# Issuing the layout of group B's bias table beside a score tile of the prompt, in place of during the second projection

## The chip, the cores and the metric

The kernel runs on one core of a Trainium2 chip. The metric is the device time of one execution in microseconds; before the change, three executions took 2215.56, 2209.62 and 2214.93 us, median 2214.93. The core has five engines with a queue of instructions each: TensorE (PE in the profile; PEld is its weight load), VectorE (DVE), ScalarE (ACT), GpSimd (POOL) and SyncE (SP), which here issues DMAs only. 16 DMA engines move the data, whichever queue issued it.

## The reference

One encoder layer, all float32, is applied to two sequences: a prompt of 1024 tokens and a sample of 512, each with 16 learned meta tokens in front.

```python
h = rmsnorm(x, norm1_g)
qa, ka, va, qb, kb, vb = split(h @ w_in)          # 1024 -> 2304 columns
qa, ka, qb, kb = per-head rmsnorm of each
oa = neighbourhood attention(qa, ka, va, rpb_a)   # group A: 8 heads, 2-D window of a 64-wide grid
ob = windowed attention(qb, kb, vb, t5, sink)     # group B: 8 heads, 2 kv heads, +-128 window
x = x + concat(rmsnorm(oa), rmsnorm(ob)) @ w_out
h = rmsnorm(x, norm2_g)
x = x + (silu(h @ w_gate) * (h @ w_up)) @ w_down  # FFN, width 2816
```

In both groups a bias depends on the distance between query and key: in group A a learned table of 15 x 31 offsets for each head, in group B the T5 buckets, with everything beyond 128 masked. In group B there is a sink logit as well. The meta keys are always visible.

## The kernel before

The work runs in stages with a common barrier behind most of them. The tokens lie in three segments of 512: two of the prompt (0 and 1) and the sample (2). The stages are: norm of segment 0, projection 0, norm 1, projection 1, attention of the prompt, norm 2, projection 2, attention of the sample, output projection ("mix"), FFN. Every product of float32 is done as three TensorE products of a high and a low part, so that all operands are split by ScalarE (high) and by VectorE or GpSimd (low).

**Projection** (`project(g)` on each engine, called with 0, 1, 2). Nine iterations: four pairs of query columns, four of keys and values, and one for group B's keys and values. In an iteration SP loads two weight tiles `wraw` of 512 KB (L602), each as soon as the tile before the last in its slot is free; ScalarE makes the high half `wh` (L972), GpSimd the low half `wl` (L796); TensorE multiplies (L354 to L356) and averages squares (L1532); ScalarE evacuates (L999, L1000) and takes the root (L1025); VectorE inverts and scales (L1284, L1294). ScalarE's `body` is the function that the diff touches: in its first iteration (`it == 0`), behind the root, it also issues a layout of a bias table.

**The bias tables.** A bias tile is a sheared copy of a short line of values: row p of it is the line shifted by p. The lines lie in DRAM (`line_a_dram`, `line_b_dram`), and DMAs from DRAM to DRAM write the sheared tables `table_a` (two halves, one for each sequence) and `table_b`, from which the bias of a head is later loaded. `lay_out_a(0)` issues 8 DMAs (L927) in projection 0, `lay_out_b` 2 DMAs (L935; 216 KB in runs of 18 values and 4608 KB in runs of 384) in projection 1, and `lay_out_a(1)` 16 DMAs beside tile 68 of the prompt's attention. All are issued by ScalarE's queue, on which they stand in order with its other instructions.

**Attention.** A sequence has 16 heads, 8 of group A and then 8 of group B; a head of the prompt has 8 tiles of 128 queries, numbered n = 0 to 127 over the sequence, each with two or three blocks of 128 keys. The engines go through the tiles in step: TensorE's scores of tile n+1 (L1576 to L1579) into one of two banks; VectorE adds the bias and finds the maximum (L1326); ScalarE takes the exponential (L1064); TensorE transposes the probabilities (L1583); ScalarE evacuates them as `pth` (`raise_p`, L1073), VectorE makes their low part `ptl` (L1333), and TensorE multiplies them with the values (L1604). ScalarE's order in `attention(seq)` is: exponential n, then what stands beside that tile, evacuation n-1, and in tile 2 of a head the copy of the next head's queries (L1057).

In each head there are side tasks. SP, in its order: the bias load of the next head, the doubling of the next head's queries (L700), and, every second head, the store and the spread of a pair's inverse sums (L705, L710). For group A the bias of a head comes through one buffer `bias_rows` (L684, 576 KB), which GpSimd adds to the mask (`masks`, L832); for group B it is loaded from `table_b` (L692, L694), the first time for head 8 after a wait on the layout's semaphore. GpSimd, in its order: copy of the meta probabilities (L856), `masks` of the next head, low half of the next head's queries (L814), again L856, meta values (L841), and every second head the scaling of a pair (L849). TensorE transposes the copied meta probabilities at L1588.

Of the kernel before, what the change touches and what calls it, by code (L numbers as in the profile page):

```python
# [64 lines left out]
def hybrid_encoder_layer(nc, x_prompt, x_sample, meta_tokens, t5_table, norm1_g, w_in, qn_a_g, kn_a_g,  # L65
# [152 lines left out]
    with ExitStack() as ctx:  # L218
        bank = [ctx.enter_context(nc.psum_tensor(f"bank{i}", [P, 512], F32)) for i in range(8)]

        def sem(name):
            return ctx.enter_context(nc.semaphore(name))
# [13 lines left out]
        line_out = sem("line_out")  # L236
# [98 lines left out]
        def wait(eng, s, v):  # L335

            if not isinstance(v, int) or v > 0:
                eng.wait_ge(s, v)
# [30 lines left out]
        def norm_tiles(g):  # L369

            first = 0 if g == 0 else 5 + 4 * (g - 1)
            src = x_of["sample"] if g == 2 else x_of["prompt"]
            t0 = 0 if g == 2 else g * SEG
            tiles = [(first + i, P, i * P, src[t0 + i * P:t0 + (i + 1) * P, :]) for i in range(4)]
            if g == 0:
                tiles.append((first + 4, META, SEG, meta_tokens[:, :]))
            return tiles
# [541 lines left out]
        def _(act):  # L919
            def lay_out_a(q):  # L920

                R, W = GEO["prompt" if q == 0 else "sample"]
                for c in range(W):
                    src = line_a_dram[3 * q, 0:1, PAD_A + (R - 1) * 3 * W - c:][0]
                    src = bass.AP(src.tensor, src.offset, [[LEN_A, 3 * NA], [-3 * W, R], [1, WIN]])
                    dst = table_a[q].rearrange("k h (r c) j -> (k h) r c j", c=W)[:, :, c, :]
                    act.dma_start(dst, src).then_inc(table_a_out[q], 16)  # L927

            def lay_out_b():

                for k0, n, off in ((0, MK, P - 1), (MK, WIN, LEN_BM + P - 1)):
                    src = line_b_dram[0, 0:1, off:][0]
                    src = bass.AP(src.tensor, src.offset, [[LEN_B, 3 * NA], [-1, P], [1, n]])
                    dst = table_b[:, :, :, k0:k0 + n].rearrange("k h p c -> (k h) p c")
                    act.dma_start(dst, src).then_inc(table_b_out, 16)  # L935
# [38 lines left out]
            def project(g):  # L974
                sq, rt = sq_of[g // 2], rt_of[g // 2]

                def body(it, kind, i):
                    if g == 0 and kind == "kvb":

                        for m, rows, _, _ in norm_tiles(1)[:3]:  # L980
                            norm_root(1, m, rows)
                    normed_slots = (0, 1) if kind == "q" else (0,)
                    j0 = normed_number(g, kind, 0, i)
                    if isinstance(it, int) and it == 0:

                        wait(act, v_turned, 5 * g)
                        wait(act, k_lo, 5 * g)

                    for slot in range(2):
                        us = units(g, kind, slot)  # L990
                        if kind != "kvb":
                            weight_hi(g, it + 1, slot, True)
                        else:
                            act.wait_ge(mm_done, 18 * g + it * 2 + slot + 1)

                        wait(act, normed, j0 - 1 if kind == "q" and slot == 0 and not isinstance(i, int) else j0)
                        if slot in normed_slots:
                            for u0, w, b, _ in us:
                                act.activation(raw[slot][:, u0:u0 + w], b[:, 0:w], ACT.Copy)  # L999
                                op = act.activation(sq[slot][:, u0:u0 + w], b[:, 0:w], ACT.Square)  # L1000
                            op.then_inc(squared, 1)
                        else:
                            wait(act, v_turned, v_number(g, kind, i))
                            n = SEG // len(us)
                            for j, (_, _, b, _) in enumerate(us):
                                src, dst = b[:, 0:n], raw[1][:, j * n:(j + 1) * n]
                                if kind == "kv":

                                    W, rows = (16 if g == 2 else 8), n // GRID
                                    src = src.rearrange("p (r t c) -> p t r c", r=rows, c=W)  # L1010
                                    dst = raw[1][:, 0:SEG].rearrange("p (t r c) -> p t r c", r=8, c=W)
                                    dst = dst[:, :, j * rows:(j + 1) * rows, :]
                                op = act.activation(dst, src, ACT.Copy)
                            if g == 0:
                                src = us[1][2][:, n:n + META].rearrange("p (o c) -> p o c", o=1)
                                op = act.activation(vtm[:, :].rearrange("p (o c) -> p o c", o=8),
                                                    src.broadcast_to((P, 8, META)), ACT.Copy)
                            op.then_inc(v_copied, 1)

                    for slot in normed_slots:  # L1020
                        act.wait_ge(mean_done, j0 + slot + 1)
                        if kind != "q":
                            wait(act, k_lo, v_number(g, kind, i))
                        for u0, w, _, mb in units(g, kind, slot):
                            op = act.activation(rt[slot][:, u0:u0 + w], mb[:, 0:w], ACT.Sqrt, bias=eps[:, :])  # L1025
                        op.then_inc(root_done, 1)
                    if kind != "q":
                        act.wait_ge(v_turned, v_number(g, kind, i) + 1)
                        for src, hi, _ in v_dests(g, kind, i):
                            op = act.activation(hi, src, ACT.Copy)  # L1030
                        if g == 0:
                            c = 4 * P if kind == "kvb" else i * P
                            op = act.activation(vmh[:, bass.ds(c, P)], bank[5][:, 0:P], ACT.Copy)
                        op.then_inc(v_hi, 1)
                        act.wait_ge(normed, j0 + 1)
                        for x, hi, _, _ in k_parts(g, kind, i):
                            op = act.activation(hi, x, ACT.Copy)
                        op.then_inc(k_hi, 1)
                    if isinstance(it, int) and it == 0 and g < 2:

                        with nc.allow_non_contiguous_dma("runs of bias lines"):
                            if g == 0:
                                act.wait_ge(line_out, 16 * 7)
                                lay_out_a(0)
                            else:
                                lay_out_b()

                pairs(act, body)
                if g:
                    phase_end(act, END_OF[f"proj{g}"])  # L1050
# [32 lines left out]
            def attention(seq):  # L1083
                first, end = HEADS_OF[seq]
                n0, n1 = TILES[seq]
                for h in (first, first + 1):
                    stage_q(h, False)
                for n in range(n0, n1 + 4):
                    if n < n1:
                        exponent(n)  # L1090
                    if n == 68:
                        with nc.allow_non_contiguous_dma("runs of bias lines"):
                            lay_out_a(1)
                    pair = pair_beside(n - 1, seq)
                    if pair is not None:
                        rows = 2 * Head(2 * pair).nt
                        act.wait_ge(rt_turned, pair + 1)
                        act.wait_ge(p_turned, min(n, n1))
                        wait(act, rt_stored, 16 * pair)
                        act.activation(rt_sb[0:rows, :], bank[2][0:rows, WIN:WIN + P], ACT.Copy  # L1100
                                       ).then_inc(rt_out, 1)
                    if n % GROUP == 2 and n - 6 >= n0:
                        raise_meta((n - 6) // GROUP)
                    if n0 <= n - 1 < n1:
                        raise_p(n - 1)
                    if n < n1:
                        h, t = where(n)
                        if t == 2 and first < h < end - 1:
                            stage_q(h + 1, True)
                phase_end(act, END_OF[f"att_{seq}"])  # L1110
# [712 lines left out]
```

## Time and profile before

| what | us |
|---|---|
| median of three runs | 2214.93 |
| the profiled execution | 2209.63 |
| its span, first to last instruction | 2207.8 |
| TensorE busy | 1958.6 (89%) |
| VectorE busy | 1051.5 (48%) |
| ScalarE busy | 667.1 (30%) |
| GpSimd busy | 507.5 (23%) |

Mean granted clock of TensorE over the span is 0.94. The last half of the span is the FFN, in which TensorE is busy throughout. Projection 1 lies at about 205 to 335 us, the prompt's attention at 336 to 574, projection 2 at 600 to 722, the sample's attention at 724 to 932.

In a timeline a row gives start and duration in us, engine, line, operation, tile written from tiles read, and in brackets how long the engine sat idle before the row and what ended that. "issue" is time in which it waited for nothing that the profile shows. A letter q behind an engine's name is its queue, which issues DMAs. Of a DMA there are two times: how long the queue took to issue it, and the time from issue to landing.

### The profile page before, as it was taken

To read this page: it belongs to the slowest core of one execution; us is meant where nothing else is said; L and a number is where in the kernel's file an instruction comes from. 1 tells how busy PE (TensorE), PEld (TensorE's weight loads), DVE (VectorE), ACT (ScalarE), POOL (GpSimd) and SP (SyncE) were. 2 spreads that over 40 slices of the span, in tenths; PEclk is the share of its full clock that TensorE was granted. 3 is DMA by queue.
4 is the path that set the end of the run, shared out by engine and by line. 5 is a ranking of instruction groups with operands and counts; after the bars stand their busy time and mean duration, and the time that the engine had idled before them with its cause. 6 is when DMAs were issued, how large, how long until landed. Compare 5 with 4: busy or idle time off the path is not lost.

```text
span 2207.8 us, 28015 instructions
## 1 busy us (share of the span) xinstructions
PE 1958.6 (89%) x9991; PEld 1646.3 (75%) x9991; DVE 1051.5 (48%) x1788; ACT 667.1 (30%) x1373; POOL 507.5 (23%) x405
## 2 busy tenths in 40 slices
PE   5896887979599466599989999999999999999998
PEld 3695567979577465568758888888888888888887
DVE  3565456757455333465553344433433444334336
ACT  3344346757434433333441111111111111111110
POOL 1231324534233432232111111121111111111110
PEclk7998998989799677789999999999999999999999
DMA  3432513343321323240011000011010000110102
GB/s 101 159 114 52 153 48 94 82 145 90 96 78 55 83 71 98 69 155 1 0 48 39 29 28 28 28 40 36 28 38 28 28 28 28 45 31 28 38 9 114
DMA packets 146718, 136.18 MB, mean 62 GB/s; under 512 B 10880, under 2 KB 133232, under 8 KB 146648
## 3 DMA queue, kind: packets, MB, share of 16 engines
q1 hardware_dynamic: 134048, 120.90, 18.2%
q10 hardware_dynamic: 12600, 14.38, 2.1%
q8 instruction: 40, 0.66, 0.1%
q14 instruction: 30, 0.25, 0.0%
HBM read 122.36 MB, written 20.98 MB: 65 GB/s over the span
## 4 chain that ended last, share of the span: by engine, by line
PE 52%; DVE 3%; issue 1%; POOL 1%; ACT 1%; ACTq 0%; POOLq 0%; DVEq 0%
PE bank L354 17%; PE bank L356 17%; PE bank L355 17%; POOL msl L892 1%; DVE h2l L1447 1%; DVE y L1458 1%; DVE h2h L1449 0%; ACT msh L1126 0%; DVE y L1388 0%; PE bank L1604 0%; PE bank L1699 0%; DVE wol L1392 0%; ACT junk L1145 0%; DVE xn L1402 0%; POOL wol L900 0%
## 5 line engine op out<-in xcount | busy, mean ns | idle before, releaser
L1458 DVE TENSOR_TENSOR y<-bank,y 128x512 f32<-128x512 f32 x528 | 359.3, 692 | 305.7 <-PE bank L356 305.7
L354 PE MATMUL bank<-h2h,gh 128*128 128x512 f32 x528 | 208.5, 395 | 7.3 <-DVE h2h L1449 5.5
L354 PE MATMUL bank<-hth,wh 128*128 128x512 f32 (+2 forms) x512 | 200.7, 392 | 8.9 <-POOLq L349 6.9
L354 PE MATMUL bank<-h2h,uh 128*128 128x512 f32 x528 | 206.3, 391 | 2.5 <-POOL ul L912 2.5
L354 PE MATMUL bank<-dh,acth 128*128 128x512 f32 x528 | 205.7, 390 | 2.6 <-issue 2.6
L355 PE MATMUL bank<-h2l,gh 128*128 128x512 f32 x528 | 206.3, 391 | 0.0
L356 PE MATMUL bank<-h2h,gl 128*128 128x512 f32 x528 | 206.2, 391 | 0.0
L356 PE MATMUL bank<-h2h,ul 128*128 128x512 f32 x528 | 206.1, 390 | 0.0
L355 PE MATMUL bank<-h2l,uh 128*128 128x512 f32 x528 | 206.0, 390 | 0.0
L356 PE MATMUL bank<-dh,actl 128*128 128x512 f32 x528 | 205.6, 389 | 0.0
L355 PE MATMUL bank<-dl,acth 128*128 128x512 f32 x528 | 205.6, 389 | 0.0
L796 POOL TENSOR_TENSOR wl<-wraw,wh 128x1024 fp32r<-128x1024 f32 x54 | 131.4, 2438 | 310.7 <-ACT wh L972 310.7
L1467 DVE TENSOR_TENSOR act_f<-bank,act_f 128x512 f32<-128x512 f32 x66 | 45.6, 692 | 319.3 <-PE bank L356 319.3
L912 POOL TENSOR_TENSOR dl<-draw,dh 128x1024 fp32r<-128x1024 f32 x22 | 52.6, 2393 | 611.2 <-ACT dh L1190 611.2
L355 PE MATMUL bank<-htl,wh 128*128 128x512 f32 (+2 forms) x512 | 187.7, 367 | 0.0
L356 PE MATMUL bank<-hth,wl 128*128 128x512 f32 (+2 forms) x512 | 186.9, 365 | 0.0
L1583 PE MATMUL bank<-ident,logit 128*128 128x128 f32 x512 | 138.7, 298 | 7.0 <-ACT logit L1064 7.0
L1284 DVE RECIPROCAL rt_p<-rt_p 128x512 f32<-128x512 f32 (+2 forms) x31 | 87.7, 2843 | 112.8 <-ACT rt_p L1025 112.8
L1216 ACT ACTIVATE acth<-act_f 128x512 fp32r<-128x512 f32 x66 | 41.7, 632 | 324.2 <-DVE act_f L1467 324.2
L1326 DVE CUSTOM_DVE_ANT_0 logit<-bank,bias 128x274 f32<-128x274 f32 (+1 forms) x192 | 100.0, 522 | 77.6 <-PE bank L1579 58.5
L1333 DVE TENSOR_TENSOR ptl<-bank,pth 128x256 fp32r<-128x256 f32 (+1 forms) x192 | 98.4, 513 | 64.2 <-ACT pth L1073 60.8
L354 PEld LDWEIGHTS bank<-hth,wh 128*128 128x128 f32 x512 | 98.5, 192 | 37.4 <-POOL wl L796 8.4
(186 smaller groups left out, 4053.2 us busy)
## 6 DMA issues: line engine op xcount, KB each, us to landing
wraw<-in_w_in SPq DMA_DIRECT2D x54, 512.0 KB, 3.9
graw<-in_w_gate SPq DMA_DIRECT2D x22, 512.0 KB, 3.9
uraw<-in_w_up SPq DMA_DIRECT2D x22, 512.0 KB, 3.9
draw<-in_w_down SPq DMA_DIRECT2D x22, 512.0 KB, 3.4
bias_rows<-table_a SPq DMA_DIRECT2D x16, 576.0 KB, 4.4
bias<-table_b SPq DMA_DIRECT2D x16, 402.0 KB, 3.5
out<-y SPq DMA_DIRECT2D x12, 512.0 KB, 3.1
table_a<-line_a_dram ACTq DMA_DIRECT2D x8, 576.0 KB
```

The costliest lines, as they stand in the source:

```text
L354: pe.matmul(out, lhs[0], rhs[0], start=start, stop=False, skip_group_check=True)
L355: pe.matmul(out, lhs[0], rhs[1], start=False, stop=False, skip_group_check=True)
L356: return pe.matmul(out, lhs[1], rhs[0], start=False, stop=stop, skip_group_check=True)
L796: pool.tensor_tensor(wl[slot][:, :, :], wraw[slot][:, :, :], f32(wh[slot][:, :, :]), ALU.subtract).then_inc(w_lo, 1)
L912: pool.tensor_tensor(lo[:, :, :], rw[:, :, :], f32(hi[:, :, :]), ALU.subtract).then_inc(s_lo, 1)
L1216: act.activation(acth[:, u * SEG:(u + 1) * SEG], act_f[:, u * SEG:(u + 1) * SEG], ACT.Copy).then_inc(act_hi, 1)
L1284: op = dve.reciprocal(rt[slot][:, u0:u0 + w], rt[slot][:, u0:u0 + w])
L1326: dve.tensor_tensor_reduce(logit[:, n % (2 * GROUP), 0:w], bank[n % 2][:, 0:w], H.bias_of(t), -1.0, 3e38, ALU.add, ALU.min, negm[:, h % 2, ...
L1333: dve.tensor_tensor(turned_to(ptl, n), bank[2 + n % 2][:, 0:k * P].rearrange("p (k c) -> p k c", c=P), f32(turned_to(pth, n)), ALU.subtrac ...
L1458: dve.tensor_tensor(yt, down_bank(t, half)[:, :], yt, ALU.add).then_inc(y_add, 1)
L1467: dve.tensor_tensor(a_, UP_BANKS[u][:, :], a_, ALU.mult).then_inc(act_done, 1)
L1583: return pe.transpose(bank[2 + n % 2][:, c * P:(c + 1) * P], logit[:, n % (2 * GROUP), MK + c * P:MK + (c + 1) * P], ident[:, :])
```

## The change

The two DMAs of `lay_out_b` are no longer issued in the first iteration of projection 1, but on the same queue in the prompt's attention, between the exponential of tile n = 12 and the evacuation of tile 11. Nothing else moves.

```diff
-                    if isinstance(it, int) and it == 0 and g < 2:
+                    if isinstance(it, int) and it == 0 and g == 0:
 
                         with nc.allow_non_contiguous_dma("runs of bias lines"):
-                            if g == 0:
-                                act.wait_ge(line_out, 16 * 7)
-                                lay_out_a(0)
-                            else:
-                                lay_out_b()
+                            act.wait_ge(line_out, 16 * 7)
+                            lay_out_a(0)
...
                     if n < n1:
                         exponent(n)
-                    if n == 68:
+                    if n in (12, 68):
                         with nc.allow_non_contiguous_dma("runs of bias lines"):
-                            lay_out_a(1)
+                            if n == 12:
+                                lay_out_b()
+                            else:
+                                lay_out_a(1)
```

## Rows read from the trace of the kernel before

**Rows 1.** Windows view, prompt's attention: stretch, length, engines' busy time, clock, DMA share, GB/s.

```profile
336.00:574.00 238.00, 201.09 (x1832) 197.67 (x1832) 159.72 (x494) 160.21 (x456) 105.90 (x152) 0.93 0.34 98
```

**Rows 2.** Timeline of SP's queue, prompt's attention: start, duration, queue, line, DMA.

```profile
364.36 0.47 SPq L700 DMA_DIRECT2D qs_p0h<-qs_p0h  x1
...
381.41 0.59 SPq L684 DMA_DIRECT2D bias_rows<-table_a  x1
...
454.13 0.48 SPq L700 DMA_DIRECT2D qs_p1h<-qs_p1h  x1
...
481.49 0.48 SPq L700 DMA_DIRECT2D qs_p0h<-qs_p0h  x1
```

**Rows 3.** Timeline of ScalarE, second projection.

```profile
215.66 0.69 ACT L1025 ACTIVATE rt_p<-bank,eps 128x512 f32<-128x512 f32 x1 [4.62 <-PE bank L1532]
215.66 4.09 ACTq L935 DMA_DIRECT2D table_b<-line_b_dram  x2
...
270.55 0.60 ACT L999 ACTIVATE raw<-bank 128x512 f32<-128x512 f32 x1 [3.39 <-DVE qm L1294]
```

**Rows 4.** Landings of weight loads issued at 222 to 230; then of all 54.

```profile
DMA to landing us min/median/max: 17.3/19.2/21.2
...
DMA to landing us min/median/max: 3.7/3.9/21.2
```

**Rows 5.** Timeline of TensorE, second projection.

```profile
222.50 1.12 PE L1532 MATMUL bank<-sq_p,head_mean 128*128 128x512 f32 x2 [1.31 <-ACT sq_p L1000]
...
243.62 2.07 PE L1532 MATMUL bank<-sq_p,head_mean 128*128 128x512 f32 x2 [7.47 <-ACT sq_p L1000]
```

**Rows 6.** Windows view, second projection.

```profile
230.00:240.00 10.00, 6.14 (x26) 4.49 (x24) 4.10 (x2) 0.69 (x1) 0.00 (x0) 0.99 0.79 225
240.00:250.00 10.00, 6.38 (x20) 4.42 (x21) 0.00 (x0) 4.40 (x7) 3.58 (x2) 0.67 0.79 227
```

**Rows 7.** Timeline of ScalarE, third projection.

```profile
617.63 0.69 ACT L1025 ACTIVATE rt_s<-bank,eps 128x512 f32<-128x512 f32 x1 [4.62 <-PE bank L1532]
...
661.21 0.60 ACT L999 ACTIVATE raw<-bank 128x512 f32<-128x512 f32 x1 [3.39 <-DVE qm L1294]
```

**Rows 8.** Timeline of ScalarE, tile 12 of the prompt's attention.

```profile
365.45 0.63 ACT L1064 ACTIVATE logit<-logit,negm 128x402 f32<-128x402 f32 x1
...
366.08 0.47 ACT L1073 ACTIVATE pth<-bank 128x384 fp32r<-128x384 f32 x1
```

**Rows 9.** Timeline of ScalarE, tile 68 of the prompt's attention.

```profile
456.15 13.03 ACTq L927 DMA_DIRECT2D table_a<-line_a_dram  x15
469.27 0.49 ACT L1073 ACTIVATE pth<-bank 128x384 fp32r<-128x384 f32 x1 [13.21 <-issue]
```

**Rows 10.** Timeline of TensorE, prompt's attention.

```profile
368.10 0.32 PE L1604 MATMUL bank<-pth,vh 128*64 128x256 f32 x1
...
393.92 0.27 PE L1588 MATMUL bank<-ident,pmeta 128*64 128x128 f32 x1
...
457.82 0.26 PE L1579 MATMUL bank<-kmeta,qs_p0l 128*128 128x18 f32 x1
470.41 0.48 PE L1604 MATMUL bank<-pth,vh 128*64 128x256 f32 x1 [12.33 <-DVE ptl L1333]
```

**Rows 11.** Timeline of ScalarE's queue, first projection.

```profile
59.80 10.83 ACTq L927 DMA_DIRECT2D table_a<-line_a_dram  x8
```

**Rows 12.** Timeline of GpSimd, prompt's attention, around the masks of head 4.

```profile
386.67 2.40 POOL L832 TENSOR_TENSOR bias<-bias_rows,mask_a 128x256 f32<-128x256 f32 x3 [3.08 <-DMA bias_rows<-table_a]
390.12 2.51 POOL L814 TENSOR_TENSOR qs_p0l<-qm,qs_p0h 64x512 fp32r<-64x512 f32 x2 [1.06 <-ACT qs_p0h L1057]
392.70 0.24 POOL L856 COPY pmeta<-logit 128x64 f32<-128x64 f32 x1
```

**Rows 13.** Landings of the two spreads of sums issued at 380.3, then at 457.2.

```profile
DMA to landing us min/median/max: 3.8/4.0/4.3
...
DMA to landing us min/median/max: 5.4/6.5/7.7
```

## The prediction

> **What bounds the kernel now.** I read the windows view first, then the timelines of the engines in the two stages that the diff touches, then DMA landing times. Over the prompt's attention TensorE is busy 201 of 238 us [rows 1]; this includes the stage's two ends and one large hole, so between them it is the engine that sets the pace, and what stops it is paid nearly in full. The head period is steady: the query copies of heads 2 and 9 were issued at 364.36 and 454.13, seven heads apart, 12.82 us each, 1.60 us a tile [rows 2]. The second projection is set by TensorE too, except in one place: there its clock falls and it waits. That place is the layout of table_b.
>
> **The part that is removed.** ScalarE's queue issues the two DMAs of the layout at 215.66 for 4.09 us together [rows 3], and moves 4.8 MB on the same DMA engines as the weight loads. The two weight loads issued while it ran landed after 17.3 and 21.2 us, where the median of all is 3.9 [rows 4]. The reader should see three losses. ScalarE does nothing else while it issues; TensorE stands 1.31 and then 7.47 us [rows 5]; the granted clock, 0.99 from 230 to 240 and 0.67 in the next 10 us, goes to half at 239.8 [rows 6], with TensorE stopped since 243.62 - 7.47 = 236.15.
>
> The third projection runs the same loop on the same shapes with no layout beside it, so it prices the sum of these. From the square root of the first pair (215.66 before, 617.63 in the third) to the evacuation of the first key and value pair (270.55 and 661.21) it takes 54.89 against 43.58 us [rows 3, 7]. The removal gives back 11.31 us. From below, the two idle rows alone are 8.8 us [rows 5]; what they leave out is the half clock and a smaller wait. I take 11.3, because both ends of the comparison are the same instructions. What is late next is only TensorE's own stream, as in the third projection.
>
> **The part that is added: the issue.** The query copy of head 2 stands in tile 10; with its doubling at 364.36 [rows 2], the exponential at 365.45 is tile 12's [rows 8], and the two DMAs go in behind it, ahead of the evacuation that now starts at 366.08. Tile 68, where the other sequence's table is laid out, has the same place in its head, and shows what follows: the 16 issues end at 469.18, ScalarE goes on at 469.27 and TensorE at 470.41, 1.14 us later [rows 9, 10]. Queued behind the issues on ScalarE are this evacuation of probabilities and the next exponentials; VectorE's low half waits for the evacuation, and TensorE's products with the values for that.
>
> At the old price of 4.09 us the issues of tile 12 end at 369.54, ScalarE goes on at 369.63, TensorE at 370.77. It would have started that product at 368.10 [rows 10]: a loss of 2.7 us. Its two ends: if both issues cost as little as an issue at tile 68, 13.03/15 or 0.87 us, they end at 367.2 and TensorE loses 0.3 us. If they stretch as the eight larger issues of table_a's first half did (10.83/8 or 1.35 us each [rows 11], 1.56 times those of tile 68), 4.09 becomes 6.4 us and the loss 5.0 us. I take 3.0 us: the old duration with a little on top, since the attention's own loads share the DMA engines. Below nothing is excluded: nothing on ScalarE is shortened here.
>
> The hole would be about 2.8 us long. The hole at 236.15 cost the clock 3.8 us after it began; the 1.31 us hole did not cost it [rows 5, 6]. I count no clock loss; if the hole reaches 5 us there is one. Its price is read at tile 68: the next query copy came at 481.49 in place of 454.13 + 12.82, so 14.5 us late, of which 12.3 is idle [rows 2, 10]; 2.2 us are the half clock.
>
> **The part that is added: the transfer.** The 4.8 MB now run beside the attention's loads for some 25 to 35 us from 368 on (in the projection the DMA share was still 0.79 from 230 to 250, up to 34 us after the issue [rows 6]). First use of table_b is head 8 at tile 64, over 80 us later, so its own landing is covered; were it not, the loss would be the whole transfer. The loads that meet it: the doubling of head 3's queries, the store and spread of the first pair's sums, and the bias rows of head 4, issued at 381.41 behind that spread on SP [rows 2]. The last one has a waiter: GpSimd starts its masks at 386.67, having waited 3.08 us for this load, which so lands after some 5.2 us [rows 12]. Behind the masks stand, in GpSimd's order, the low half of head 4's queries (390.12) and the copy of the meta probabilities (392.70, 0.24 long) [rows 12], and TensorE transposes that copy at 393.92 [rows 10]. Between the masks' end (389.07) and 390.12 there is 1.05 us, and behind the copy 0.98: 2.0 us of slack. What the load loses beyond that, TensorE waits.
>
> How late is it? The same spread of sums, issued at 457.2 beside the other table's layout, landed after 5.4 and 7.7 us in place of 3.8 and 4.3 [rows 13]: 1.6 to 3.4 us late. Weight loads, of smaller pieces, lost up to 17.3 us [rows 4]. The bounds for the bias rows are therefore 0 and 16 us late (a landing at 21.2). The spread is the nearest: the bias rows queue behind it, so its 3.4 us is theirs too, and I add little for their own part, for by then most of the layout has gone: 4.0 us late. Loss 4.0 - 2.0 = 2.0 us. Later loads (head 5's rows at some 394 us) meet at most the tail; nothing for these.
>
> The Trainium skill (DMA: Bandwidth & Descriptors, "Queues, rings and completion order") says that each DMA engine takes turns between the queues that have work, a packet at a time, and under "Issuing engines are not separate DMA queues" that issuing from another engine saves only the sequencer's time. That speaks against this change: the bytes move into a stage with loads of its own. Worked out as an estimate from that page, taking turns at most doubles a landing of 5.2 us, so 5.2 us late, 3.2 us lost, and the whole change gives 5.1 us. The weight loads' landings were worse than double; no row shows the taking of turns itself.
>
> **The sum.** -11.3 + 3.0 + 2.0 = -6.3 us. The profiled execution took 2209.63 us (span 2207.8), hence 2203.3. It lies 5.3 us under the median of the three runs shown (2209.62, 2214.93, 2215.56); the same 6.3 us off that median gives 2208.6 us.
>
> **The rivals.**
>
> No collision: the bias rows land within GpSimd's 2.0 us of slack. For it: that is only 0.6 us more than the 1.6 by which the first spread was late. Against it: they queue behind the second, which was 3.4 late. -11.3 + 3.0 = -8.3: 2206.6 us.
>
> A long issue: the two DMAs hold ScalarE for 6.4 us and the hole pulls the clock down. For it: the stretched issues of table_a's first half, and loads in flight; against it: those 8 were queued one behind another. -11.3 + 5.0 + 2.2 + 2.0 = -2.1: 2212.8 us.
>
> Slower: the bias rows of head 4 land as the weight loads did, after 21.2 us. The place is GpSimd's masks for head 4; the price 16 - 2.0 = 14.0 us of TensorE, with the clock at half after it (2.2). -11.3 + 3.0 + 14.0 + 2.2 = +7.9: 2222.8 us. It outweighs the gain from a delay of 8.1 us on, a landing over 13.3 us. For it: the only loads seen beside this very table lost that much. Against it: the spread beside a layout lost at most 3.4, and the layout is partly done when the bias rows come.
>
> The projection doesn't recover: its waits have another cause, and only ScalarE's 4.09 us goes. For it: nothing but that the two wait rows name ScalarE and not the DMA. Then about -4.1 + 5.0 = +0.9: 2215.8 us.
>
> **How the numbers follow.** Forecast 0.54, no collision 0.18, long issue 0.16, slower 0.07, projection not recovered 0.05. I call 0.3% (6.6 us, about what a measurement of this kernel can tell from no change) the bound. No collision lies beyond it; the forecast (own range 3 to 8 us gained) lies just inside it, and nearly half of its weight falls beyond. So faster 0.18 + 0.26 = 0.44. Slower takes its rival and a little of the last one's: 0.08. The rest, 0.48, is the same. The range goes from the no-collision case less half of the runs' spread of 5.9 us (about 2203.5) to the long issue and a little more (2214); the slower rival and the unrecovered projection, 0.12 together, lie outside.
>
> **What would show it.** In the profile after: weight loads of the second projection all near 3.9 us and no clock loss there, 43.6 us between the two instructions compared; a gap of TensorE of about 2.8 us at tile 14 whose releaser is VectorE's low half, with ScalarE's idle put to issue for about 4 us; GpSimd's wait for the bias rows of head 4 longer by 4 us, and a TensorE wait of about 2 us for the meta probabilities' copy or what follows it. It is wrong if the weight loads stay slow, if the issues take well over 5 us, or if other waits (query doubling, head 5's rows) appear in the attention.

## The result and the profile after

20 executions of each kernel were timed side by side: median 2223.73 us (2216.06 to 2228.77) after, 2215.24 (2209.21 to 2221.96) before. The ratio is 1.0029, 95% interval 1.0017 to 1.0041; it is that of the means, 2222.2 and 2215.8 us, while the medians lie 8.5 us apart. The kernel is slower by 0.3%, about 6.4 us, where 6.3 us of gain were forecast. The profiled execution after took 2216.06 us, its span is 2214.3.

Where the time went can be read from SP's queue alone, since SP issues the first load of each stage. The table has the time from the second projection's first streamed weight load to the attention's mask load, from there to the next norm's first load, and so on. The last two columns belong to experiments told below.

| stage, us | before | after | early copy, before | early copy, after |
|---|---|---|---|---|
| second projection | 139.71 | 128.73 | 144.92 | 129.04 |
| prompt's attention | 239.19 | 254.81 | 235.05 | 253.73 |
| norm and third projection | 149.14 | 148.90 | 148.40 | 149.54 |
| sample's attention, to the load of y | 217.09 | 216.89 | 197.51 | 201.38 |

The projection gives 11.0 us back, the attention takes 15.6. (The projection starts 2.3 us later in the profile after, 197.88 for 195.61; the eight profiles of the experiments lie at 196.2 to 200.3, so that is no part of the change.)

The projection is as it should be. Landings of its weight loads in the profile after (issued from 143 to 350), the windows, and the two instructions of ScalarE compared in [rows 3, 7]:

```profile
DMA to landing us min/median/max: 3.7/3.9/5.2
```

```profile
230.00:240.00 10.00, 10.00 (x42) 7.44 (x41) 5.51 (x4) 5.26 (x8) 4.57 (x2) 1.00 0.25 74
240.00:250.00 10.00, 10.00 (x43) 7.62 (x41) 7.56 (x4) 3.07 (x5) 2.66 (x2) 1.00 0.23 63
```

```profile
218.28 0.69 ACT L1025 ACTIVATE rt_p<-bank,eps 128x512 f32<-128x512 f32 x1 [4.61 <-PE bank L1532]
...
261.87 0.60 ACT L999 ACTIVATE raw<-bank 128x512 f32<-128x512 f32 x1 [3.39 <-DVE qm L1294]
```

They are 43.59 us apart, as in the third projection (43.58), and TensorE has no gap in these 20 us, where it had lost over a third of them [rows 6].

In the attention TensorE has three waits that it did not have. The view of waits of the profile after, TensorE, 350 to 410 us (what waited, for what; total, times, longest):

```profile
PE bank L1604 <- DVE ptl L1333: 3.8, 1, 3.8
PE bank L1576 <- issue: 3.6, 1, 3.6
PE bank L1588 <- POOL pmeta L856: 2.4, 1, 2.4
```

The first is the hole behind the issues. ScalarE's timeline shows its cause:

```profile
357.50 0.78 ACTq L935 DMA_DIRECT2D table_b<-line_b_dram  x1
358.03 0.19 ACT L1061 ACTIVATION_READ_ACCUMULATOR logit<-logit,negm 128x1 f32 x1
358.32 4.56 ACTq L935 DMA_DIRECT2D table_b<-line_b_dram  x1
362.98 0.49 ACT L1070 ACTIVATE pth<-bank 128x384 fp32r<-128x384 f32 x1 [4.76 <-issue]
```

The second issue took 4.56 us, the two 5.38, where they had taken 4.09 in the projection [rows 3].

The second wait is put to issue, which means that the profile shows no releaser. SP's timeline and the landing times show one: the doubling of head 3's queries was issued at 375.48 and landed 8.5 us later, at 383.98, and the first scores of head 3 start at 384.11. The two fences are TensorE's timeline with both gaps, and SP's:

```profile
364.12 0.47 PE L1604 MATMUL bank<-pth,vh 128*64 128x256 f32 x1 [3.82 <-DVE ptl L1333]
...
384.11 0.55 PE L1576 MATMUL bank<-kall,qs_p1h 128*128 128x256 f32 x1 [3.60 <-issue]
```

```profile
375.48 0.47 SPq L700 DMA_DIRECT2D qs_p1h<-qs_p1h  x1
376.38 0.83 SPq L705 DMA_DIRECT2D rt_dram<-rt_sb  x1
384.45 1.11 SPq L710 DMA_DIRECT2D rinv_q<-rt_dram  x2
385.61 0.59 SPq L684 DMA_DIRECT2D bias_rows<-table_a  x1
```

The next doublings in the profile after land after 2.8 or 2.9 us. In the same fence the store of 8 KB at 376.38 holds SP until 384.45; in the view of SP's waits it is 7.2 us, before 1.8. Only then could the bias rows of head 4 go out, and they landed after 10.0 us, so that GpSimd waited 13.77 us and finished the copy of the meta probabilities too late, the third wait:

```profile
395.63 2.41 POOL L832 TENSOR_TENSOR bias<-bias_rows,mask_a 128x256 f32<-128x256 f32 x3 [13.77 <-DMA bias_rows<-table_a]
398.12 2.48 POOL L814 TENSOR_TENSOR qs_p0l<-qm,qs_p0h 64x512 fp32r<-64x512 f32 x2
400.66 0.24 POOL L856 COPY pmeta<-logit 128x64 f32<-128x64 f32 x1
```

Both longer gaps also cost the clock. The windows after (the granted clock, as a share of full speed, is the third number from the end):

```profile
360.00:365.00 5.00, 1.18 (x8) 1.06 (x7) 1.49 (x5) 1.89 (x5) 0.47 (x1) 0.74 1.19 112
365.00:370.00 5.00, 5.00 (x31) 5.00 (x30) 3.30 (x11) 2.46 (x9) 2.58 (x4) 0.58 0.78 127
...
380.00:385.00 5.00, 1.40 (x11) 1.29 (x9) 1.94 (x6) 1.16 (x5) 0.24 (x1) 0.79 0.79 246
385.00:390.00 5.00, 5.00 (x31) 5.00 (x32) 2.13 (x7) 1.99 (x6) 0.00 (x0) 0.53 1.07 239
```

The sum is taken from one doubling to the next on SP, 12.82 us apart before [rows 2]: in the profile after they stand at 356.40, 375.48, 394.59, 409.98 and 422.83, so the heads took 19.08, 19.11, 15.39 and 12.85. The excess is 6.3, 6.3 and 2.6 us: the hole of 3.8, the doubling's wait of 3.6 and the bias rows' 2.4. What is left over beside the first two, 2.4 and 2.7 us, is put down to the clock; it is a difference and was not measured by itself.

### The profile page after: what moved, and what is told of

It reads as the page before. It is cut to its first block, busy times and chain, and to the rows that moved or that the text cites. A ratio compares the mean times of both kernels' runs of the same rounds, so it can differ in the third digit from the quotient of the medians.

```text
span 2214.3 us, 28015 instructions
## 1 busy us (share of the span) xinstructions
PE 1964.8 (89%) x9991; PEld 1652.7 (75%) x9991; DVE 1052.2 (48%) x1788; ACT 667.4 (30%) x1373; POOL 508.1 (23%) x405
## 4 chain that ended last, share of the span: by engine, by line
PE 52%; DVE 3%; issue 1%; POOL 1%; ACT 1%; ACTq 0%; POOLq 0%; DVEq 0%
PE bank L354 17%; PE bank L356 17%; PE bank L355 17%; POOL msl L892 1%; DVE h2l L1447 1%; DVE y L1458 1%; DVE h2h L1449 0%; ACT msh L1126 0%; DVE y L1388 0%; PE bank L1604 0%; PE bank L1699 0%; DVE wol L1392 0%; ACT junk L1145 0%; DVE xn L1402 0%; POOL wol L900 0%
## 5 line engine op out<-in xcount | busy, mean ns | idle before, releaser
L354 PEld LDWEIGHTS bank<-h2h,gh 128*128 128x128 f32 x528 | 99.5, 188 | 35.6 <-DVE h2h L1449 10.0
```

Source lines behind the costliest of these rows:

```text
L354: pe.matmul(out, lhs[0], rhs[0], start=start, stop=False, skip_group_check=True)
```

## The experiments

Each was timed in five rounds beside the kernel before, eight kernels in all. A ratio is to the kernel before.

**The two DMAs apart.**

```diff
-                    if n in (12, 68):
+                    if n in (8, 12, 68):
...
-                            if n == 12:
-                                lay_out_b()
+                            if n < 68:
+                                lay_out_b((0,) if n == 8 else (1,))
```

> The small DMA of the layout is issued beside tile 8 and the large one beside tile 12, so that the second no longer stands right behind the first on ScalarE's queue. Theory A (three separate losses in the changed kernel: ScalarE held 5.35 us, with the clock, some 6 us; the doubling of head 3's queries, with the clock, some 6 us; head 4's bias rows 2.4 us): each issue takes about 0.8 us, TensorE stops less than 1 us at tile 14, its clock stays up there; the other two losses stay. The time is about 6 us under the changed kernel, so about that of the kernel before (-3 to +3 us). Rival B (the long issue is itself the transfer's doing: the DMA engines are busy with the attention's loads and take descriptors slowly): the large issue still takes 3 us or more, the hole stays, and the time stays some 4 to 8 us above the kernel before.

Ratio 0.9986 (0.9972 to 1.0): 0 to 6 us faster than before, some 9.5 us under the changed kernel by the two ratios, where 6 were expected; the attention of the profiles is 6.3 us shorter. ScalarE's queue, then TensorE's waits from 350 to 410 us, of this kernel:

```profile
351.88 0.78 ACTq L935 DMA_DIRECT2D table_b<-line_b_dram  x1
...
358.85 0.74 ACTq L935 DMA_DIRECT2D table_b<-line_b_dram  x1
```

```profile
PE bank L1588 <- POOL pmeta L856: 4.1, 1, 4.1
PE bank L1576 <- issue: 2.4, 1, 2.4
```

The large DMA costs 0.74 us to issue when it doesn't follow the small one (3072 runs of 72 bytes; its own 3072 runs have 1536) at once, and the hole (L1604) is gone. Rival B falls: the issue was long because of the DMA ahead of it on its queue. Of the attention's excess 9.3 us are left (248.48 us). The doubling's wait is shorter by 1.2 us, the bias rows' longer by 1.7, a first sign that these two are not added but overlap.

**The query copy earlier, and its control.** Both have the same edit, one on the changed kernel and one on the kernel before.

```diff
-                        if t == 2 and first < h < end - 1:
+                        if t == 0 and first < h < end - 1:
                             stage_q(h + 1, True)
```

> The changed kernel, with the copy of the next head's queries (and so their doubling) in tile 0 of a head in place of tile 2, some 3.2 us earlier. Theory A: the doubling of head 3's queries still lands late (some 8 us), but 3.2 of the 3.6 us that TensorE waited for it are gone, and the clock doesn't fall for it: 5 to 6 us less than the changed kernel, if the early copy costs nothing by itself (its control is the kernel before with the same edit): difference to the control 0 to +2 us. Rival B (TensorE's wait of 3.6 us, which the profile puts to issue, has another cause, such as GpSimd's low half or the scores' banks): the wait stays, and the difference to the control stays at +6 us or more.

> Control for the early copy of the queries: the kernel before, with the copy in tile 0 of a head in place of tile 2. Both theories: no wait in the prompt's attention hangs on this copy, so within 2 us of the kernel before; if ScalarE is pressed at tile 0, up to 5 us slower, which then is taken off the other.

Ratios 0.9921 (0.9907 to 0.9934) and 0.989 (0.9873 to 0.9907). The control was a miss in a welcome way: by its stages, nearly 20 us of its gain lie in the sample's attention (217.09 to 197.51). TensorE's waits at a head's first scores there are for GpSimd's low half of the copied queries, which follows that copy. They fell from 57.5 to 52.3 us, one of 3.6 us that is put to issue went, and the stage's 856 products took 115.6 us in place of 127.1, at a mean granted clock of 0.80 in place of 0.75.

For the question asked, the difference of the two stays at 0.3%, some 7 us, which is what rival B expected; by the table the move here costs 18.7 us in the attention and gives 15.9 in the projection. But the reason is not rival B's. TensorE's waits in the changed kernel with the early copy, 350 to 410 us:

```profile
PE bank L1588 <- POOL pmeta L856: 13.7, 1, 13.7
PE bank L1604 <- DVE ptl L1333: 3.2, 1, 3.2
```

The wait at the first scores (L1576) is gone. The edit moves GpSimd's low half of these queries as well, but in the profile after that was done at 378.11, 2.4 us before TensorE stood, so the wait was for the doubling:

```profile
375.59 2.52 POOL L814 TENSOR_TENSOR qs_p1l<-qm,qs_p1h 64x512 fp32r<-64x512 f32 x2 [5.84 <-ACT qs_p1h L1054]
```

In its place the wait for the copy of the meta probabilities grew from 2.4 to 13.7 us: GpSimd stood 18.52 us for head 4's bias rows. Some 6.3 us of the growth are what TensorE no longer lost ahead of that wait. The rest is that the rows came later still: SP stood 8.6 us at the store (7.2 in the profile after, 1.0 in the control), and the load landed after 13.4 us (10.0 in the profile after, 5.5 in the control). Theory A, three separate losses, falls as to the last two. The doubling's wait lay in the shadow of a later one.

**The bias rows first.** The same kernel, with one change in SP's order.

```diff
+                    if h == 3:
+                        spread_sums(0)
                     if first < h < end - 1:
                         double_q(h + 1)
-                    if h % 2 == 0 and h > first:
+                    if h % 2 == 0 and h > first and h != 2:
                         spread_sums(h // 2 - 1)
```

> The changed kernel with the early copy of the queries, and with head 4's bias rows issued ahead of the first pair's store and spread on SP, not behind them. Theory C (what ends last in the changed kernel's collision is SP's chain for head 4: a store of 8 KB that takes 7 to 9 us beside the layout in place of 1.8, SP standing at it, and the bias rows queued behind; the stalls of TensorE before it only lie in its shadow): the bias rows go out some 10 us earlier, TensorE's wait of 13.7 us for the meta probabilities falls to under 3 us, and the prompt's attention shortens from 253.7 to 237 to 243 us; the time falls 11 to 16 us below the same kernel without this edit. Rival D (the bias rows' own landing beside the layout is what is late, 10 us and more wherever they are issued): the wait stays at 6 us or more and the time falls by less than 8 us.

Ratio 0.9882 (0.9862 to 0.9901); the attention went from 253.73 to 241.83 us. SP's queue, then TensorE's waits from 350 to 410 us:

```profile
371.35 0.59 SPq L684 DMA_DIRECT2D bias_rows<-table_a  x1
374.84 0.34 SPq L705 DMA_DIRECT2D rt_dram<-rt_sb  x1
382.05 1.11 SPq L710 DMA_DIRECT2D rinv_q<-rt_dram  x2
```

```profile
PE bank L1606 <- DVE ptl L1335: 2.8, 1, 2.8
PE bank L1578 <- issue: 1.0, 1, 1.0
```

The bias rows go out at 371.35 in place of 383.67. Their landing still takes 10.3 us, as rival D has it:

```profile
DMA to landing us min/median/max: 10.3/10.3/10.3
```

But they land some 15 us earlier, GpSimd waits 1.05 us for them in place of 18.52, and the 13.7 us are gone. The store still holds SP for 7 us, but nobody waits behind it. Theory C holds for the wait and for the stage (237 to 243 us expected). Two of its points don't. The timed runs gave some 9 us (0.9921 to 0.9882), between its 11 to 16 and rival D's less than 8. And the place behind the store was only half of the lateness: over the control, the store had taken 7.6 us more and the landing 7.9. The new place in SP's order makes room for both. What is left over the control, 6.8 us, holds the hole of the issue (2.8), its clock and a wait of 1.0 for a doubling.

**The hold alone.** The kernel before, with this ahead of tile 12's evacuation and no transfer added:

```diff
+                    if n == 12:
+                        for x in range(18):
+                            act.activation(rt_sb[0:16, :], ident[0:16, :], ACT.Copy).then_inc(held, 1)
+                            act.wait_ge(held, x + 1)
```

> The kernel before (layout in the second projection), with ScalarE held for some 5 to 6 us beside tile 12 by 18 small copies in a chain, and no transfer: the price of the issue alone. Theory A: TensorE stops 3.5 to 4.5 us at tile 14, its clock falls to half afterwards, and the stage takes 5 to 7 us more; +5 to +7 us. Rival (a hold alone is made good, since the engines behind have idle time): +1 to +3 us.

Ratio 1.0032 (1.0019 to 1.0045), 7.1 us; the attention took 247.29 us, 8.1 more. ScalarE's and TensorE's timelines:

```profile
368.57 6.08 ACT L1094 ACTIVATE rt_sb<-ident 16x128 f32<-16x128 f32 x18
```

```profile
375.82 0.48 PE L1609 MATMUL bank<-pth,vh 128*64 128x256 f32 x1 [5.08 <-DVE ptl L1338]
```

A hold of 6.08 us stops TensorE 5.08 us, 1.0 less, about as the prediction took it; the other 3 us are put down to the clock, 0.78 in 370 to 375 us and 0.53 in 375 to 380. The stop and the time lie a little over what was expected, as does the hold. Nothing of it beyond that 1.0 us is made good later, and the rival falls. This hold, 0.7 us longer than the two issues, costs by itself what the whole change cost on balance.

**The layout in pieces.** Eight pieces of 16 rows of every head's table, and the small DMA, each beside a tile in which ScalarE has idle time.

```diff
+                    at_b = [8 * h + x for h in range(5) for x in (5, 7)][:9]
+                    if n in at_b or n == 68:
...
+                                piece_b(8 if n == 5 else at_b.index(n) - 1)
```

> The layout leaves the second projection as in the change, but goes out in nine pieces (the 216 KB one and eight of 576 KB, 16 rows of each head's table each), beside tiles 5 and 7 of the first five heads, where ScalarE has some idle time. Theory A: each issue holds ScalarE 0.8 us, TensorE's slack of about 1 us covers it; a piece of 576 KB is gone before the next doubling is due; 9 to 11 us under the kernel before. Rival B (what costs is the traffic, 4.8 MB beside the attention's loads, wherever it is cut): the loads stay late by the same sum, 2 to 8 us above the kernel before.

Ratio 0.9962 (0.9948 to 0.9977), 8.4 us faster, a little short of what was expected. ScalarE's queue shows a likely cause:

```profile
343.31 0.78 ACTq L935 DMA_DIRECT2D table_b<-line_b_dram  x1
346.16 3.17 ACTq L935 DMA_DIRECT2D table_b<-line_b_dram  x1
356.73 0.75 ACTq L935 DMA_DIRECT2D table_b<-line_b_dram  x1
```

The piece that came 2 us behind the small DMA took 3.17 us to issue, all later ones 0.75. The attention is 2.5 us over that of the kernel before, in place of 15.6. Rival B, that the traffic costs the same wherever it is cut, falls.

**All of it, and its control.** The pieces with the small DMA a head ahead of the next, the sample's layout in 16 single DMAs, and the early copy:

```diff
+                    at_b = [5] + [8 * h + x for h in range(1, 5) for x in (5, 7)]
+                    at_a = [8 * h + x for h in range(8, 16) for x in (5, 7)]
+                    if n in at_b + at_a:
...
-                        if t == 2 and first < h < end - 1:
+                        if t == 0 and first < h < end - 1:
```

> The change carried on: group B's layout in nine pieces beside tiles 5 to 39 (the small one eight tiles ahead of the next), the sample's layout in 16 single DMAs beside tiles 69 to 127 in place of all at tile 68, and the early copy of the queries. Theory A: against the kernel before with only the last two of these, the second projection is 11 to 16 us shorter and the prompt's attention at most 4 us longer. Against the kernel before: 24 us from the early copy, 12 to 14 from the hole at tile 68, 8 to 12 from the projection: 44 to 50 us faster. Rival: nine pieces of traffic cost what one does, and the attention takes back 9 us or more.

> Control for that one: the kernel before, with the early copy of the queries and the sample's layout in 16 single DMAs, and group B's layout where it was, in the second projection. 24 us from the copy and 12 to 14 from the hole at tile 68: 35 to 39 us faster than the kernel before. If single issues hold ScalarE at tiles where it has no idle time, 28 to 34.

Ratios 0.9779 (0.976 to 0.9798) and 0.9826 (0.9805 to 0.9847), medians 2167.15 and 2179.41 us. With the layout in pieces the second projection took 128.31 us for the control's 137.09, and the attention 221.31 for 220.74: the move then costs 0.6 us and gives 8.8, where 11 to 16 were expected. Of TensorE's waits from 345 to 460 us only this is left:

```profile
PE bank L1585 <- ACT logit L1061: 0.5, 3, 0.2
```

This kernel beats both, by 2.2% the one before. In their time both came out within what was expected (49 us for 44 to 50; 38.6 for 35 to 39).

## Why the prediction was wrong, step by step

- *The removal, 11.3 us.* Right: 11.0 in the profile, with the weight loads, the clock and the 43.6 us as foretold. Its size isn't fixed, though: with the layout in it, the second projection took 139.71, 144.92, 139.17 and 137.09 us in the four profiles, without it 128.3 to 129.0 in six.
- *The issue, 3.0 us.* Wrong in size: 6.3 us. The duration carried over was 4.09 us and came out at 5.38; that TensorE loses about 1 us less than ScalarE was right (3.82 of 4.76). "I count no clock loss" failed: the hole of 3.8 us cost some 2.4 us of it. It would have failed at the size foretold as well: in the kernel with the bias rows first a hole of 2.8 us took the clock to 0.74 from 360 to 365 us and to 0.57 in the next 5. (The 3.8 us that the prediction read at 236.15 are 3.65 by its own two times.) This was the long issue rival in its mechanism, at 6.3 where that had 7.2.
- *The transfer.* Here the step failed that decided the sign: for all that the transfer does 2.0 us were taken, and it cost 8.9 (6.3 and 2.6). "The last one has a waiter" left one out: the doubling of head 3's queries, named in the sentence before, has one too, TensorE itself, and was costed at nothing. In the trace of before it was issued at 377.18 us and landed after 2.9, and the first scores that need it start at 382.07, 2.0 us later; beside the layout its landing took 5.6 us more, 3.6 of which became TensorE's wait. Price 6.3 us with the clock. The prediction has "query doubling" among the signs of its being wrong, but without a price. To cost the doubling alone wouldn't have been enough, as the early copy shows: where its wait is gone, that for the bias rows takes its place. (The first load from `table_b` is issued at 433.43 in the trace of before, 68 us after tile 12's exponential and not over 80; nothing hung on that.)
- *The bias rows, 2.0 us.* Right in what TensorE waited (2.4), but by luck: the load was not 4.0 us late but went out behind a store that took 5.4 us more, and then took 4.8 us more to land. Counted from the doubling's issue, GpSimd started on the rows 10.7 us later than before (20.15 for 9.49); 6.3 of these TensorE had already lost at the doubling, 2.0 were the slack, and 2.4 are left. With no other stall ahead of it the price would have been 8.7 us by this sum; in the kernel with the early copy, where the load came later still, it was 13.7. The slower rival named this place and bounded its landing rightly (up to 21.2 us, here 10.0), but took only the landing and not SP's wait before it.
- *The rule of the Trainium skill* (DMA: Bandwidth & Descriptors, "Queues, rings and completion order"), that engines take turns, gave an estimate of twice the landing: the bias rows' 10.0 us for 5.2 agree; their 13.4 for 5.5 with the early copy, the doubling's 8.5 for 2.9 and SP's 7.2 for 1.8 at the store are more than that, so that "at most doubles" did not hold here. Weighed on every load that the transfer meets, not on the one load, this estimate would have shown the doubling's wait, though at 0.9 us (2.9 us late, 2.0 of slack) in place of 3.6.
- *The sum.* -11.0 + 6.3 + 6.3 + 2.6, and 0.8 us more from the attention's mask load to head 2's doubling, is +5.0; by the table of stages it is +4.6, and the timed runs give +6.4.

What stays open: why SP stands some 7 us for a store of 8 KB beside the layout. That it does is seen in four kernels (7.2, 6.5, 8.6 and 6.8 us; 1.8 before); no experiment took it apart. Nor is it shown why the bias rows landed after 10.0 us in one of these kernels and after 13.4 in another.

## What to carry to other kernels

A transfer that is moved meets every load of the stage that it enters: list each with its landing time and the slack of its waiter, doublings and small stores too, and follow the queue's order behind each wait. Stalls that come one behind another hide each other, so taking away the one that the waits name may bring out the next at its full price; price each by an experiment that removes the others. Here the large layout cost least when it was cut into pieces that the idle time of the issuing engine and the slack of the loads can hold.

## What was not expected of the hardware

- The time to issue a DMA depends on what was issued just ahead on the same queue. The large DMA took 0.74 us alone; right behind the small one of 3072 runs of 72 bytes 3.27 (before), 4.56 (after) and 3.01 to 3.54 in five other kernels, and a piece of 384 runs of 1536 bytes, some 2 us behind the small one, 3.17. The same piece some 2 us behind another such piece took 0.76, so it is not the distance alone. Whether the number of runs or their length does it is not shown.
- A small store suffered more in proportion than a large load: SP stood 7.2 us in place of 1.8 for 8 KB, and 576 KB landed after 10.0 us in place of 5.2.
- A wait of the same length may or may not cost the clock. The 2.4 us for the doubling with the two DMAs apart did (0.91 from 375 to 380 us, 0.75 in the next 5); the 2.4 us for the bias rows in the profile after did not (1.00 from 395 to 410).
- Four of ten profiles have the layout in the second projection; the slowest weight load there took 21.2, 25.8, 19.4 and 19.3 us.
